# The last 512 tokens' gate projection moved between the Fourier products, and the attention tables loaded row by row

## The chip, the cores and the metric

The kernel runs on one core of a Trainium2 chip. The metric is the device time of one execution in microseconds, the median of three runs. All work of the core shares one TensorE (PE), one VectorE (DVE), one ScalarE (ACT), one GpSimd (POOL), the SyncE (SP), which in this kernel issues nearly all transfers, and 16 DMA engines.

## The reference

One layer of a hybrid encoder on 2048 tokens of 1024 channels, in float32, cut here to the parts that matter:

```python
h = rms_norm(x, norm1_g)
u_f, q, k, v, g = split(h @ w_in)                 # 512, 512, 512, 512, 2 x 1024 columns
g = sigmoid(g.reshape(b, s, 2, 1024) + b_gate)
a = fourier_mix(u_f) @ w_fa                       # real part of a 2-D DFT, 4 groups of 128 channels
n = neighbourhood_attention(q, k, v, rpb) @ w_nb  # 8 heads; window of 8 rows x 16 columns, with a bias table
x = x + (g[0] * a + g[1] * n) @ w_out
up = depthwise_conv(rms_norm(x) @ w_up); val, gate = split(up)
x = rms_norm(x + (silu(gate) * val) @ w_down)
```

## The kernel before

Five stages run one after the other with a barrier between them: input projection, Fourier mixing, attention, mixer output, feed-forward. Each stage is a block in which every engine has its own instruction list, written out by hand; order between engines is kept by semaphores alone. SP works through its list in order, and so a transfer waits for every wait that stands ahead of it in that list.

Every float32 product is made of three matmuls on a head and a tail (`SPLIT`): an operand is rounded to a head, and the tail is the operand less the head. Weights are read raw (512 KB a tile), DVE casts the head (`head`, L226, and L279 in the gate loop), and POOL subtracts for the tail (`tail`, L202).

**Input stage** (`input_phase`). The normalised, turned input stays in SBUF as `hT`, head and tail, 128 KB of each partition. The gates are the last part: 16 weight tiles of 128 output channels, each against four blocks of 512 tokens. One tile and block is 24 matmuls of 128x512 (`tile`, L357). ACT adds the bias and takes the sigmoid on the way from PSUM to a stage buffer (L335), and SP stores it to `gT` in HBM (L189). The loop over the gates is a hardware loop (`Fori`), two weight tiles a turn.

**Fourier stage** (`fourier_phase`). SP loads `u` in two halves of 256 columns, the position table (`traw`, 2 MB) and the channel table (L479 to L482). DVE does a 16-point transform of each half (`dft16`, L525 and L528); ACT and POOL split its result into `Y` (L620, L508). PE multiplies it by the position table, 48 matmuls of 128x256 for each group (L666); ACT and DVE split that into `X` (L628, L583); PE multiplies by the channel table, 18 matmuls (L676); ACT and DVE write the group's output (L635, L594, L599), and SP stores it (L495). SP's list also makes the shifted bias tables for the attention: a zeroed table, the `rpb` values put into it, and 48 small copies of 31 KB (L484 to L491).

**Attention stage** (`attention_phase`). For each of 8 heads SP loads q and k twice (4 x 512 KB), nine bias tables (9 x 256 KB, L785) and the values (16 x 64 KB, L793); for head 0 the window mask (2.3 MB, L787) stands between bias and values. ACT casts q and k (L883), POOL and DVE subtract for the tails (L819, L860), DVE adds the mask to each bias table (L857), and 128 tiles of scores follow: PE scores (L938), DVE adds the bias and takes the maximum (L836), ACT exponential (L889), PE transpose (L948), DVE copy (L844), PE values (L960).

Of the kernel before, what the change touches and what calls it, by code (L numbers as in the profile page):

```python
# [44 lines left out]

class Pool:
# [18 lines left out]
def input_phase(nc, x, w_in, norm_g, b_gate, eye, u_out, qT_out, v_out, kT_out, gT_out):  # L65
# [6 lines left out]
    with ExitStack() as ctx:  # L72
        m = Pool(nc, ctx, "in")
        hT = m.sb("hT", [P, 2, KD, SEQ], F32R)
# [8 lines left out]
        bias_now = m.sb("bias_now", [P, 2])  # L83
# [22 lines left out]
        bias_ready = m.sem("bias_ready")  # L106
        evac_done = m.sem("evac_done")
        stored = m.sems("stored", STAGES)

# [6 lines left out]
        free_at = [0, 0, 0, 0, 0, 0, 20, 24, 16, 16, 16, 16, 28, 32, 52, 56]  # L116
        ng_evac = 16 + 16 + 16 + 16
# [7 lines left out]
        def _(sp):  # L125
# [46 lines left out]
            def load_gate(t):  # L172
                sp.dma_start(wraw[:, t % RAW], w_in[16 + t]).then_inc(w_in_raw[t % RAW], 16)

            for q in range(4):
                if q >= 2:
                    sp.wait_ge(w_tail, UQVK + q - 2 - 1)
# [4 lines left out]
            with sp.Fori(0, NG // 2 - 1) as i:  # L182
                for j in range(2):
                    sp.wait_ge(w_tail, i * 2 + (UQVK + j + 1))
                    sp.dma_start(wraw[:, j], w_in[bass.ds(i * 2 + (18 + j), 1)].rearrange("o p k c -> (o p) k c")
                                 ).then_inc(w_in_raw[j], 16)
                    for b in range(NBLK):
                        sp.wait_ge(evac_done, i * 8 + (ng_evac + 4 * j + b + 1))
                        sp.dma_start(gT_out[bass.ds((i * 2 + j) * P, P), b * BLK:(b + 1) * BLK],  # L189
                                     stage[:, b]).then_inc(stored[b], 16)  # L190
            n = ng_evac + 4 * (NG - 2)
            for t in range(NG - 2, NG):
                for b in range(NBLK):
                    store(n, gT_out[t * P:(t + 1) * P, b * BLK:(b + 1) * BLK])
                    n += 1
            for s in range(STAGES):
                sp.wait_ge(stored[s], 16 * (n // STAGES))

        @block.gpsimd
        def _(pool):  # L200
# [4 lines left out]
            for t in range(UQVK):  # L205
                pool.wait_ge(w_head, t + 1)
                tail(t, slot[t])
            with pool.Fori(0, NG // 2) as i:
                for j in range(2):
                    pool.wait_ge(w_head, i * 2 + (UQVK + j + 1))  # L210
                    tail(j, 4 + j)

        @block.vector
        def _(dve):
# [7 lines left out]
            def head(t):  # L222
                dve.wait_ge(w_in_raw[t % RAW], 16 * (t // RAW + 1))
                if free_at[t]:
                    dve.wait_ge(mm_done, free_at[t])
                nc.vector.tensor_copy(w[:, 0, slot[t]], wraw[:, t % RAW]).then_inc(w_head, 1)  # L226
# [18 lines left out]
            def h_tails(t):  # L245
                for g in range(2):
                    dve.wait_ge(head_done, 2 * t + g + 1)
                    ks, at = slice(4 * g, 4 * g + 4), slice(t * P, (t + 1) * P)
                    nc.vector.tensor_tensor(hT[:, 1, ks, at], ps[:, 2 * (t % 2) + g].rearrange("p (k q) -> p k q", q=P),  # L249
                                            f32(hT[:, 0, ks, at]), ALU.subtract).then_inc(tail_done, 1)  # L250
# [20 lines left out]
            for t in range(6, UQVK):  # L271
                head(t)
            with dve.Fori(0, NG // 2) as i:
                for j in range(2):
                    dve.wait_ge(evac_done, i * 8 + (60 + 4 * j))
                    nc.vector.tensor_copy(bias_now[:, j:j + 1], gbias[:, bass.ds(i * 2 + j, 1)]).then_inc(bias_ready, 1)
                    dve.wait_ge(w_in_raw[j], i * 16 + 16 * (UQVK // 2 + 1))
                    dve.wait_ge(mm_done, i * 8 + (60 + 4 * j))
                    nc.vector.tensor_copy(w[:, 0, 4 + j], wraw[:, j]).then_inc(w_head, 1)  # L279

        @block.scalar
        def _(act):
# [17 lines left out]
            def h_heads(t):  # L300
                act.wait_ge(x_turned, t + 1)
                for g in range(2):
                    nc.scalar.activation(hT[:, 0, 4 * g:4 * g + 4, t * P:(t + 1) * P],
# [25 lines left out]
            with act.Fori(0, NG // 2) as i:  # L329
                for j in range(2):  # L330
                    act.wait_ge(bias_ready, i * 2 + (j + 1))
                    for b in range(NBLK):
                        act.wait_ge(mm_done, i * 8 + (ng_evac + 4 * j + b + 1))
                        act.wait_ge(stored[b], i * 32 + 16 * (ng_evac // 4 + j))
                        nc.scalar.activation(stage[:, b], ps[:, 4 * j + b], ACT.Sigmoid,  # L335
                                             bias=bias_now[:, j:j + 1]).then_inc(evac_done, 1)

        @block.tensor
        def _(pe):
            pe.wait_ge(const_in, 48)  # L340

            def slab(n, t):
# [3 lines left out]
                for k in range(KD):  # L346
                    for a, b in SPLIT:
                        last = nc.tensor.matmul(ps[:, bank(n)], hT[:, a, k, t * P:(t + 1) * P], w[:, b, 0:4, k],  # L348
# [4 lines left out]
            def tile(bank, s, b, first_wait):  # L353
                pe.wait_ge(evac_done, first_wait)
                for k in range(KD):
                    for a, c in SPLIT:
                        last = nc.tensor.matmul(ps[:, bank], w[:, a, s, k], hT[:, c, k, b * BLK:(b + 1) * BLK],  # L357
# [37 lines left out]
            with pe.Fori(0, NG // 2) as i:  # L395
                for j in range(2):
                    pe.wait_ge(w_tail, i * 2 + (UQVK + j + 1))
                    for b in range(NBLK):
                        tile(4 * j + b, 4 + j, b, i * 8 + (ng_evac + 4 * j + b - BANKS + 1))


# [17 lines left out]
def fourier_phase(nc, u, pos_table, chan_table, fnT_out, rpb, padded, shifted):  # L419
# [14 lines left out]
    CW = 256  # L434
# [6 lines left out]
    USES = XB + 6  # L441
    with ExitStack() as ctx:
# [9 lines left out]
        traw = m.sb("traw", [P, A, 2 * P])  # L452
        tab = m.sb("tab", [P, 2, A, 2 * P], F32R)
        craw = m.sb("craw", [P, 2, P])
        ctab = m.sb("ctab", [P, 2, 2, P], F32R)
        X = m.sb("X", [P, 2, 2 * XB, 2, P], F32R)
        real = m.sb("real", [P, 2, BLK])
        out = m.sb("out", [P, 1, SEQ])
        zero = m.sb("zero", [REL_R * 4, P])
        ps = m.banks()  # L460

        zeroed, filled, placed, shifted_done = (m.sem(x) for x in ("zeroed", "filled", "placed", "shifted_done"))
        tab_in, u_in = m.sem("tab_in"), m.sems("u_in", CHUNKS)
# [6 lines left out]
        stored = m.sem("stored")  # L470

# [5 lines left out]
        def _(sp):  # L477
            u_v = u.rearrange("(a b) c -> b a c", b=P)
            sp.dma_start(ub[:, 0], u_v[:, :, 0:CW]).then_inc(u_in[0], 16)  # L479
            sp.dma_start(craw[:, :], chan_table).then_inc(tab_in, 16)  # L480
            sp.dma_start(traw[:, :], pos_table).then_inc(tab_in, 16)
            sp.dma_start(ub[:, 1], u_v[:, :, CW:2 * CW]).then_inc(u_in[1], 16)  # L482
            sp.wait_ge(zeroed, 1)
            sp.dma_start(padded.rearrange("h r (x c) -> (h r x) c", x=1).rearrange("(p y) c -> p (y c)", y=2),  # L484
                         zero[:, :]).then_inc(filled, 16)
            sp.wait_ge(filled, 16)
            sp.dma_start(padded[:, PAD_R:PAD_R + RPB_R, PAD_C:PAD_C + RPB_C], rpb).then_inc(placed, 16)
            sp.wait_ge(placed, 16)
# [1591 lines left out]
```

## Time and profile before

| | us |
|---|---|
| median of the runs (lowest, highest) | 3009.2 (3006.93, 3011.0) |
| the profiled execution's own time | 3011.05 |
| span of its trace | 3009.2 |
| PE busy, share of the span | 2726.6, 91% |
| DVE / ACT / POOL busy | 1411.5 / 894.0 / 863.9 |
| input stage, by SP's first transfers | 0 to 742.67 |
| Fourier stage | 742.67 to 860.87 |
| attention, from its first transfer to its last product | 860.87 to 1176 |
| mixer output and feed-forward | 1176 to 3009.2 |

PE's share in forty equal slices of the span, in tenths, where 9 is 90% or more, and the clock that it was granted:

```profile
PE   6999999998238997899994999997999999999997
PEclk9999999999669998999997999998999999999999
```

Each slice is 75.2 us. PE is full in the first nine after the start, falls to 2 and 3 tenths in the tenth and the eleventh after that (slices 11 and 12, the Fourier stage and the beginning of the attention) and is full again from there, with three short dips.

### The profile page before, as it was taken

Reading aid. Unit: us, or ns where it says so; the run is one execution under the profiler, and the core shown is the slowest. Engines: PE = TensorE matmul, PEld = TensorE weight load, DVE = VectorE, ACT = ScalarE, POOL = GpSimd, SP = SyncE. Lnnn points to the kernel's source line nnn. Section 1 sums busy time; section 2 is a strip of 40 time slices with the busy share of each in tenths; the row PEclk is TensorE's granted clock in tenths of the full one; section 3 lists DMA queues with packets and bytes.
Section 4 is the critical chain, followed back from the end, with each engine's and each line's share of the span. In section 5 each row is a group of like instructions: output and inputs, shape, how many; then the busy total and the mean of one; then the engine's idle time right before and its main releaser. Section 6 shows DMA issues by size and latency. Waiting matters only on the chain. (4 is left out here: it accounts for less than half of the span.)

```text
span 3009.2 us, 34345 instructions
## 1 busy us (share of the span) xinstructions
PE 2726.6 (91%) x12792; PEld 2265.5 (75%) x12792; DVE 1411.5 (47%) x2231; ACT 894.0 (30%) x1598; POOL 863.9 (29%) x477
## 2 busy tenths in 40 slices
PE   6999999998238997899994999997999999999997
PEld 5888888886237885677873788886888887888886
DVE  4300000000838886643445899998655554131232
ACT  3211111111225663122113444444222223343332
POOL 1020001010312232532222666665000003554553
PEclk9999999999669998999997999998999999999999
DMA  4322122222257762665544777777666665554653
GB/s 138 95 95 71 61 69 77 70 72 90 78 142 175 187 179 87 196 184 165 183 137 158 266 279 275 275 275 244 218 223 220 221 223 196 180 198 147 204 174 112
DMA packets 242518, 499.29 MB, mean 166 GB/s; under 512 B 65476, under 2 KB 86720, under 8 KB 239040
## 3 DMA queue, kind: packets, MB, share of 16 engines
q1 hardware_dynamic: 223424, 480.52, 49.3%
q10 hardware_dynamic: 18944, 16.78, 1.6%
q8 instruction: 92, 1.51, 0.2%
q14 instruction: 58, 0.48, 0.0%
HBM read 326.24 MB, written 172.52 MB: 166 GB/s over the span
## 5 line engine op out<-in xcount | busy, mean ns | idle before, releaser
L357 PE MATMUL in_psum<-in_hT,in_w 128*128 128x512 f32 x2304 | 522.6, 389 | 0.0
L357 PEld LDWEIGHTS in_psum<-in_hT,in_w 128*128 128x128 f32 x2304 | 432.5, 188 | 89.8
L1999 PE MATMUL ff_psum<-ff_w,ff_hid 128*128 128x512 f32 x2112 | 479.5, 389 | 2.1 <-POOL ff_w L1591 2.0
L1999 PEld LDWEIGHTS ff_psum<-ff_w,ff_hid 128*128 128x128 f32 x2112 | 396.3, 188 | 85.2 <-POOL ff_w L1591 2.4
L1591 POOL TENSOR_TENSOR ff_w<-ff_st,ff_w 128x512 fp32r<-128x512 f32 x176 | 249.8, 1429 | 635.0 <-ACT ff_w L1835 634.6
L1591 POOL TENSOR_TENSOR ff_w<-ff_wraw,ff_w 128x512 fp32r<-128x512 f32 x154 | 270.5, 1758 | 239.4 <-ACT ff_w L1835 239.4
L1960 PE MATMUL ff_psum<-ff_h,ff_w 128*128 128x512 f32 x1056 | 247.5, 394 | 27.3 <-DVE ff_h L1658 27.1
L202 POOL TENSOR_TENSOR in_w<-in_wraw,in_w 128x1024 fp32r<-128x1024 f32 x32 | 77.1, 2413 | 622.1 <-DVE in_w L226 311.4
L1960 PEld LDWEIGHTS ff_psum<-ff_h,ff_w 128*128 128x128 f32 x1056 | 200.6, 190 | 70.7 <-POOL ff_w L1591 28.1
L1960 PE MATMUL ff_psum<-ff_h,ff_again 128*128 128x512 f32 x1056 | 244.9, 391 | 3.5 <-DVE ff_h L1658 3.5
L1960 PEld LDWEIGHTS ff_psum<-ff_h,ff_again 128*128 128x128 f32 x1056 | 199.3, 189 | 45.4 <-issue 3.9
L1256 PE MATMUL mo_psum<-mo_act,mo_w 128*128 128x512 f32 x768 | 190.0, 405 | 41.7 <-POOL mo_act L1107 22.0
L1716 DVE TENSOR_TENSOR ff_hid<-ff_kraw,ff_hid 128x1024 fp32r<-128x1024 f32 x44 | 55.2, 1254 | 328.8 <-ACT ff_hid L1877 328.7
L1256 PEld LDWEIGHTS mo_psum<-mo_act,mo_w 128*128 128x128 f32 x768 | 145.3, 193 | 84.0 <-POOL mo_w L1102 26.8
L1979 PE MATMUL ff_psum<-ff_h2c,ff_w 128*128 128x512 f32 x792 | 189.1, 397 | 13.5 <-POOL ff_w L1591 13.5
L1979 PE MATMUL ff_psum<-ff_h2c,ff_again 128*128 128x512 f32 x792 | 188.9, 397 | 8.3 <-DVE ff_h2c L1658 6.8
L1979 PEld LDWEIGHTS ff_psum<-ff_h2c,ff_w 128*128 128x128 f32 x792 | 152.0, 192 | 47.1 <-POOL ff_w L1591 15.2
L348 PE MATMUL in_psum<-in_w,in_hT 128*128 128x512 f32 x768 | 180.5, 394 | 5.8 <-DVE in_hT L249 5.8
L1979 PEld LDWEIGHTS ff_psum<-ff_h2c,ff_again 128*128 128x128 f32 x792 | 152.1, 193 | 41.6 <-issue 6.4
L1271 PE MATMUL mo_psum<-mo_wo,mo_mixed 128*128 128x512 f32 x768 | 177.4, 391 | 1.6 <-DVE mo_mixed L1163 1.6
L1862 ACT ACTIVATE ff_vg<-ff_c,ff_param 128x1024 f32<-128x1024 f32 x88 | 109.6, 1246 | 222.2 <-DVE ff_c L1682 191.4
L348 PEld LDWEIGHTS in_psum<-in_w,in_hT 128*128 128x128 f32 x768 | 144.5, 190 | 35.9 <-DVE in_hT L249 6.2
(167 smaller groups left out, 3448.5 us busy)
## 6 DMA issues: line engine op xcount, KB each, us to landing
split<-ff_w SPq DMA_DIRECT2D x154, 512.0 KB, 3.4
ff_again<-split SPq DMA_DIRECT2D x154, 512.0 KB, 4.0
ff_st<-in_w_down_dram SPq DMA_DIRECT2D x176, 256.0 KB, 3.0
ff_wraw<-in_w_up_dram SPq DMA_DIRECT2D x44, 512.0 KB, 5.5
hidden<-ff_c SPq DMA_DIRECT2D x44, 512.0 KB, 2.9
ff_kraw<-hidden SPq DMA_DIRECT2D x44, 512.0 KB, 4.6
at_bias<-shifted SPq DMA_DIRECT2D x72, 256.0 KB
in_wraw<-in_w_in_dram SPq DMA_DIRECT2D x32, 512.0 KB, 3.9
```

What stands on the lines that cost most here:

```text
L202: nc.gpsimd.tensor_tensor(w[:, 1, s], wraw[:, t % RAW], f32(w[:, 0, s]), ALU.subtract).then_inc(w_tail, 1)
L348: last = nc.tensor.matmul(ps[:, bank(n)], hT[:, a, k, t * P:(t + 1) * P], w[:, b, 0:4, k], start=(k == 0 and (a, b) == SPLIT[0]), stop=(k ...
L357: last = nc.tensor.matmul(ps[:, bank], w[:, a, s, k], hT[:, c, k, b * BLK:(b + 1) * BLK], start=(k == 0 and (a, c) == SPLIT[0]), stop=(k = ...
L1256: last = nc.tensor.matmul(ps[:, 2 * (n % 2) + branch], w[:, a, s % 2, k], act_s[:, c, k], start=(k == ks[0] and (a, c) == SPLIT[0]), stop= ...
L1271: last = nc.tensor.matmul(ps[:, 4 + half], mixed[:, a, k, t * P:(t + 1) * P], wo[:, c, k, half * SPH:(half + 1) * SPH], start=(k == 0 and ...
L1591: nc.gpsimd.tensor_tensor(split_out(i, 1), parts(i), f32(split_out(i, 0)), ALU.subtract).then_inc(w_tail, 1)
L1716: T.tensor_tensor(hid[:, 1, n % 2], kraw[:, :, :], f32(hid[:, 0, n % 2]), ALU.subtract).then_inc(k_tail, 1)
L1862: nc.scalar.activation((val, gate)[r], c[:, n % 2, r], ACT.Identity, scale=taps(t, 1), bias=taps(t, 3)).then_inc(centred, 1)
L1960: last = nc.tensor.matmul(bank(n, j), weights(i)[:, a, q * P:(q + 1) * P], h1[:, k, q, b], start=(k == 0 and (a, b) == SPLIT[0]), stop=(k ...
L1979: last = nc.tensor.matmul(bank(n, P2 + s), weights(i)[:, a, k * P:(k + 1) * P], h2c[:, s, k, b], start=(k == 0 and (a, b) == SPLIT[0]), st ...
L1999: last = nc.tensor.matmul(ps[:, 4 * (1 - half) + t], hid[:, a, (b * PAIRS + pair) % 2, q, t * P:(t + 1) * P], weights(i)[:, e], start=(r = ...
```

## The change

1. **Gates.** In the input stage the gate tiles are now multiplied with the first three token blocks only (`GB = 3`), in a written-out loop. The last block's `hT` lives in a buffer of its own, `hB`, which outlives the stage. Each split gate weight tile (head and tail, 1 MB) is stored to a new scratch `gate_w` in HBM.
2. **Fourier stage.** It reads the 16 split tiles back through a ring of three buffers (`gw`), and PE does the 16 missing tile-and-block products between the Fourier products, into two banks of PSUM kept for them; the Fourier products cycle through six banks (`FB`) instead of eight. `u` comes in four chunks of 128 columns, each with its own `dft16` just ahead of its group. ACT takes the sigmoids and stores them on its own queue.
3. **Attention.** The mask comes in nine pieces on ACT's queue, three of them first; the values of head 0 stand behind the first three bias tables instead of behind all nine and the mask; DVE starts on the first row of tables when that row is there; for head 0 ACT casts k ahead of q.
4. The feed-forward stage uses fewer semaphores for the same waits; `load_y` gets one more wait (for the loads before it). These are not shown.

```diff
 # input stage, SP
+            def store_gate_w(t):
+                sp.wait_ge(w_tail, UQVK + t + 1)
+                at_least(sp, gate_stored, 16 * t)
+                sp.dma_start(gate_w[t], f32(w[:, :, slot[UQVK + t]])).then_inc(gate_stored, 16)
...
+            for t in range(NG):
+                store_gate_w(t)
+                if t + 2 < NG:
+                    load_gate(t + 2)
+                for b in range(GB):
                     store(n, gT_out[t * P:(t + 1) * P, b * BLK:(b + 1) * BLK])
 # input stage, PE
-            with pe.Fori(0, NG // 2) as i:
-                for j in range(2):
-                    pe.wait_ge(w_tail, i * 2 + (UQVK + j + 1))
-                    for b in range(NBLK):
-                        tile(4 * j + b, 4 + j, b, i * 8 + (ng_evac + 4 * j + b - BANKS + 1))
+            for t in range(NG):
+                pe.wait_ge(w_tail, UQVK + t + 1)
+                for b in range(GB):
+                    tile(n % BANKS, slot[UQVK + t], b, n - BANKS + 1)
+                    n += 1
 # Fourier stage
-    CW = 256
+    CW = 128
+    FB = BANKS - 2
+    NG, GRING = 2 * KD, 3
...
+            def load_gate_w(t):
+                at_least(sp, gate_mm, t - GRING + 1)
+                sp.dma_start(f32(gw[:, t % GRING]), gate_w[t]).then_inc(gw_in[t % GRING], 16)
...
             dft16(0)
-            dft16(1)
             for g in range(FNET_GROUPS):
+                if g + 1 < CHUNKS:
+                    dft16(g + 1)
                 group(g)
 # Fourier stage, ACT
+            def gates(*tiles):
+                for t in tiles:
+                    act.wait_ge(gate_mm, t + 1)
+                    nc.scalar.activation(sig[:, t % 2], ps[:, FB + t % 2], ACT.Sigmoid,
+                                         bias=gbias[:, t:t + 1]).then_inc(gate_out, 1)
+                    act.wait_ge(gate_out, t + 1)
+                    at_least(act, gate_stored, 16 * t)
+                    act.dma_start(gT_out[t * P:(t + 1) * P, SEQ - BLK:SEQ], sig[:, t % 2]).then_inc(gate_stored, 16)
 # Fourier stage, PE
+            def gates(*tiles):
+                for t in tiles:
+                    pe.wait_ge(gw_in[t % GRING], 16 * (t // GRING + 1))
+                    at_least(pe, gate_out, t - 1)
+                    for k in range(KD):
+                        for a, b in SPLIT:
+                            last = nc.tensor.matmul(ps[:, FB + t % 2], gw[:, t % GRING, a, k], hB[:, b, k],
...
 # attention, SP, head 0
+                if h == 0:
+                    load_bias(0, 0)
+                    load_values(0)
+                    load_bias(0, 1)
+                    load_bias(0, 2)
+                    return
...
-                if h == 0:
-                    sp.dma_start(window[:, :], mask).then_inc(const_in, 16)
 # attention, DVE
-                dve.wait_ge(bias_in[h % 2], 16 * NB * (h // 2 + 1))
+                if h == 0 and kind < KINDS:
+                    dve.wait_ge(first_in, 32 * KINDS)
+                elif h % 2:
+                    dve.wait_ge(bias_in[1], 16 * NB * (h // 2 + 1))
+                else:
+                    dve.wait_ge(bias_in[0], 32 * (NB - KINDS) + 16 * NB * (h // 2))
 # attention, ACT
+            load_mask(0)
             for part in range(2 * PARTS):
-                qk_head(0, part)
+                qk_head(0, (part + PARTS) % (2 * PARTS))
+            load_mask(1)
+            load_mask(2)
```

PE's list in the Fourier stage, whose rows say line, operation, output and inputs, shape and count. Before, the first three groups:

```order
L666 MATMUL ft_psum<-ft_tab,ft_Y 128x256 x48
L676 MATMUL ft_psum<-ft_X,ft_ctab 128x512 x12
L676 MATMUL ft_psum<-ft_X,ft_ctab 128x128 x6
L666 MATMUL ft_psum<-ft_tab,ft_Y 128x256 x48
L676 MATMUL ft_psum<-ft_X,ft_ctab 128x512 x12
L676 MATMUL ft_psum<-ft_X,ft_ctab 128x128 x6
```

The same place of PE's list now, with `in_hB` the kept token block and `ft_gw` the ring of weights:

```order
L734 MATMUL ft_psum<-in_hB,ft_gw 128x512 x96
L749 MATMUL ft_psum<-ft_tab,ft_Y 128x256 x48
L734 MATMUL ft_psum<-in_hB,ft_gw 128x512 x24
L761 MATMUL ft_psum<-ft_X,ft_ctab 128x512 x12
L761 MATMUL ft_psum<-ft_X,ft_ctab 128x128 x6
L734 MATMUL ft_psum<-in_hB,ft_gw 128x512 x48
L749 MATMUL ft_psum<-ft_tab,ft_Y 128x256 x48
L734 MATMUL ft_psum<-in_hB,ft_gw 128x512 x48
L761 MATMUL ft_psum<-ft_X,ft_ctab 128x512 x12
L761 MATMUL ft_psum<-ft_X,ft_ctab 128x128 x6
L749 MATMUL ft_psum<-ft_tab,ft_Y 128x256 x48
```

Four gate tiles (96 matmuls) stand ahead of the first Fourier product, and one or two tiles between most others. Further down the list (not shown) the position products of the third and of the fourth group follow the channel product of the group before directly, and three tiles stand at the end.

SP's list at the start of the Fourier stage, before:

```order
L479 DMA ft_u<-u 128x16x256
L480 DMA ft_craw<-in_chan_table_dram 128x256
L481 DMA ft_traw<-in_pos_table_dram 128x4096
L482 DMA ft_u<-u 128x16x256
L484 DMA padded<-ft_zero 124x128
```

SP's list there now, down to the second batch of bias-table copies:

```order
L496 DMA ft_u<-u 128x16x128
L493 DMA ft_gw<-gate_w 128x2048
L509 DMA ft_craw<-in_chan_table_dram 128x256
L510 DMA ft_traw<-in_pos_table_dram 128x4096
L511 DMA ft_gbias<-in_b_gate_dram 128x16
L493 DMA ft_gw<-gate_w 128x2048
L496 DMA ft_u<-u 128x16x128
L493 DMA ft_gw<-gate_w 128x2048
L516 DMA padded<-ft_zero 124x128
L519 DMA padded<-in_rpb_dram 8x15x31
L496 DMA ft_u<-u 128x16x128 x2
L493 DMA ft_gw<-gate_w 128x2048
```

The second weight tile stands behind the 2 MB table, the fourth (the last row) behind two waits for the padded table and behind the last two chunks of `u`; 16 small copies then stand ahead of each of the next two.

SP's list at the start of the attention, before:

```order
L774 DMA at_kraw<-kT 64x2048
L785 DMA at_bias<-shifted 128x1x512 x9
L787 DMA at_window<-in_mask_dram 128x4608
L793 DMA at_vs<-v 32x8x64 x16
L774 DMA at_qraw<-qT 64x2048
```

And now:

```order
L894 DMA at_kraw<-kT 64x2048
L877 DMA at_bias<-shifted 128x1x512 x3
L884 DMA at_vs<-v 32x8x64 x16
L877 DMA at_bias<-shifted 128x1x512 x6
L894 DMA at_qraw<-qT 64x2048
```

The mask is gone from SP's list; it stands on ACT's. The number of bytes ahead of head 1's q and k (the last row) is the same over both queues.

## Rows read from the trace of the kernel before

**Rows 1.** Windows: from:to length, PE PEld DVE ACT POOL busy, clock, DMA share, GB/s.
```profile
0.00:739.00 739.00, 715.25 (x3200) 592.78 (x3200) 80.89 (x176) 132.21 (x217) 77.33 (x36) 1.00 0.24 80
742.67:789.45 46.78, 0.00 (x0) 0.00 (x1) 38.43 (x35) 7.75 (x4) 20.13 (x4) 0.50 0.55 163
789.45:857.00 67.55, 43.60 (x264) 39.55 (x264) 42.35 (x71) 19.80 (x34) 9.03 (x2) 0.82 0.16 53
860.87:882.60 21.73, 0.00 (x0) 0.00 (x0) 4.62 (x1) 5.55 (x9) 4.50 (x1) 0.50 0.81 182
882.60:924.00 41.40, 16.71 (x74) 14.05 (x75) 13.22 (x34) 8.29 (x22) 1.13 (x1) 0.60 0.79 179
```

**Rows 2.** Waits between 739 and 925 us.
```profile
PE ft_psum L666 <- POOL ft_Y L508: 50.5, 1, 50.5
PE at_psum L938 <- DVE at_kl L860: 28.4, 1, 28.4
PE ft_psum L676 <- DVE ft_X L583: 21.2, 4, 11.2
DVE at_bias L857 <- DMA at_window<-in_mask_dram: 18.5, 1, 18.5
```

**Rows 3.** The gate loop: its matmuls by line, then timeline rows of two weight tails.
```profile
L357 PE MATMUL in_psum<-in_hT,in_w 128*128 128x512 f32 x420 | 95.4, 389 | 0.0
...
653.72 2.40 POOL L202 TENSOR_TENSOR in_w<-in_wraw,in_w 128x1024 fp32r<-128x1024 f32 x1 [19.27 <-DVE in_w L279]
...
697.24 2.40 POOL L202 TENSOR_TENSOR in_w<-in_wraw,in_w 128x1024 fp32r<-128x1024 f32 x1 [19.27 <-DVE in_w L279]
```

**Rows 4.** Timeline (start, us, what) from the last gate to the Fourier end.
```profile
739.05 0.69 ACT L335 ACTIVATE in_stage<-in_psum,in_bias_now 128x512 f32<-128x512 f32 x1 [4.75 <-PE in_psum L357]
742.67 0.39 SPq L479 DMA_DIRECT2D ft_u<-u  x1
...
750.89 4.49 DVE L528 TENSOR_TENSOR ft_st<-ft_u 128x2048 f32<-128x2048 f32 x2 [7.96 <-DMA ft_u<-u]
756.77 0.42 ACT L612 ACTIVATE ft_ctab<-ft_craw 128x256 fp32r<-128x256 f32 x1 [17.03 <-DMA ft_traw<-in_pos_table_dram]
...
763.23 0.79 SPq L487 DMA_DIRECT2D padded<-in_rpb_dram  x1
765.55 31.59 SPq L491 DMA_DIRECT2D shifted<-padded  x48
...
843.21 5.95 PE L666 MATMUL ft_psum<-ft_tab,ft_Y 128*128 128x256 f32 x48
850.55 3.68 PE L676 MATMUL ft_psum<-ft_X,ft_ctab 128*128 128x512 f32 x18 [1.39 <-DVE ft_X L583]
```

**Rows 5.** Windows while PE worked again, and in its next pause.
```profile
793.00:795.00 2.00, 2.00 (x19) 2.00 (x18) 2.00 (x3) 0.60 (x1) 0.00 (x0) 0.97 0.31 49
801.00:805.00 4.00, 0.00 (x0) 0.00 (x0) 3.97 (x13) 0.00 (x0) 0.00 (x0) 0.50 0.00 0
```

**Rows 6.** ACT's and POOL's split of the transform, by line: count, busy us, mean ns.
```profile
L508 POOL TENSOR_TENSOR ft_Y<-ft_u,ft_Y 128x2048 fp32r<-128x2048 f32 x4 | 18.8, 4707 | 42.4 <-ACT ft_Y L620 42.4
...
L620 ACT ACTIVATE ft_Y<-ft_u 128x2048 fp32r<-128x2048 f32 x4 | 7.5, 1906 | 25.6 <-DVEq L557 12.2 <-DVEq L577 7.9 <-PE ft_psum L666 5.6
```

**Rows 7.** Timeline of the attention's start.
```profile
863.74 10.75 SPq L785 DMA_DIRECT2D at_bias<-shifted  x9
873.61 2.19 ACT L883 ACTIVATE at_qs<-at_qraw 128x512 fp32r<-128x512 f32 x4 [18.58 <-DMA at_kraw<-kT]
...
877.86 26.60 SPq L793 DMA_DIRECT2D at_vs<-v  x16
...
904.57 0.50 SPq L774 DMA_DIRECT2D at_qraw<-qT  x1
...
916.91 0.63 ACT L883 ACTIVATE at_qs<-at_qraw 128x512 fp32r<-128x512 f32 x1 [9.52 <-DMA at_kraw<-kT]
```

**Rows 8.** SP's timeline of head 7's values.
```profile
1114.25 17.75 SPq L793 DMA_DIRECT2D at_vs<-v  x16
```

More of the change, by code:

```diff
@@ L43, with at_least @@
 SPLIT = ((0, 0), (0, 1), (1, 0))
+def at_least(engine, sem, value):
+    if value > 0:
+        engine.wait_ge(sem, value)
 class Pool:
@@ L203, in tail @@
                                         ALU.subtract).then_inc(w_tail, 1)
-            for t in range(UQVK):
+            for t in range(UQVK + NG):
                 pool.wait_ge(w_head, t + 1)
                 tail(t, slot[t])
[L208 to L211, printed above, removed]
         @block.vector
@@ L270, in _ @@
                     head(4 + t)
-            for t in range(6, UQVK):
+            for t in range(6, UQVK + NG):
                 head(t)
[L273 to L279, printed above, removed]
         @block.scalar
@@ L328, in _ @@
                 n += 1
[L329 to L336, printed above, removed]
+            for t in range(NG):
+                for b in range(GB):
+                    evac(n, ACT.Sigmoid, bias=gbias[:, t:t + 1])
+                    n += 1
         @block.tensor
@@ L455, in fourier_phase @@
         ctab = m.sb("ctab", [P, 2, 2, P], F32R)
+        with ExitStack() as first:
+            traw = Pool(nc, first, "ft").sb("traw", [P, A, 2 * P])
         X = m.sb("X", [P, 2, 2 * XB, 2, P], F32R)
@@ L634, in group @@
                         act.wait_ge(mirror_done, n - 1)
[L635 removed]
+                    nc.scalar.activation(real[:, n % 2, 0:w * P], ps[:, (USES * g + XB + 2 * q) % FB, 0:w * P],
                                          ACT.Copy, scale=ORTHO).then_inc(real_done, 1)
[L638 to L642 removed]
+            def gates(*tiles):
[6 more added lines that the diff above has]
+                    act.dma_start(gT_out[t * P:(t + 1) * P, SEQ - BLK:SEQ], sig[:, t % 2]).then_inc(gate_stored, 16)
+            gates(0, 1)
+            heads(0)
+            gates(2, 3)
+            spectrum(0)
+            gates(4)
+            heads(1)
+            reals(0)
+            gates(5, 6)
+            spectrum(1)
+            gates(7, 8)
+            heads(2)
+            reals(1)
+            spectrum(2)
+            gates(9, 10)
+            heads(3)
+            reals(2)
+            spectrum(3)
+            gates(11, 12)
+            reals(3)
+            gates(13, 14, 15)
+            act.wait_ge(gate_stored, 16 * NG)
         @block.tensor
@@ L909, in turn, with load_mask @@
                     ps[:, TB].rearrange("p (j b c) -> p j b c", b=QR, c=QC)[:, :, ::-1], ACT.Copy).then_inc(evac, 1)
+            def load_mask(i):
+                for kind in range(i * KINDS, (i + 1) * KINDS):
+                    act.dma_start(window[:, kind], mask[:, kind]).then_inc(bias_in[0] if i else first_in, 16)
+            load_mask(0)
             for part in range(2 * PARTS):
-                qk_head(0, part)
+                qk_head(0, (part + PARTS) % (2 * PARTS))
+            load_mask(1)
+            load_mask(2)
             for n in range(-4, N + 1):
```

244 lines of the change are left out of this document (149 added, 95 removed).

## The prediction

> **What bounds the kernel now.** I read the page's forty slices first: PE is busy 91% of the span, so the time is PE's work plus the stretches in which it has none. Then the windows by stage. Up to 739 us PE is busy and at full clock [rows 1]. From SP's first Fourier transfer at 742.67 to 789.45 it does nothing; from there to 857 it works 43.6 of 67.6 us, at a mean clock of 0.82 of full; in the first 21.7 us of the attention it again does nothing, and in the next 41.4 it works 16.7. The reader should see there one stage with PE full and next to it two starts with PE empty. The waits name the causes: 50.5 us for the split of the first transform, 21.2 us in four waits for the spectrum's tails, 28.4 us at the attention's start and on DVE 18.5 us for the mask [rows 2]. The gate loop has no idle time at all (0.0 in its row), so what is taken from it comes off in full [rows 3].
>
> **What the input stage loses.** Two tails of gate weights two tiles apart begin at 653.72 and 697.24 us, so eight tile-and-block products take 43.52 us, 5.44 each [rows 3]. Sixteen go: 16 x 5.44 = 87.0 us. The additions hide under PE. A weight tile now lasts 3 x 5.44 = 16.3 us. The cast and tail of the next one start when the tile two before it is done; the tail takes 2.4 us [rows 3], so with a cast of 1 us at most some 13 us are spare. The store of a split tile (1 MB) stands on SP ahead of the next raw load and of three stage stores; DMA share is 0.24 in this stage [rows 1], and 17 MB more over the 48 x 5.44 = 261 us of gates adds 64 GB/s to the 80. ACT has four stage buffers of 5.44 us each before it would wait. If that cover failed, a late tile would cost the excess over 13 us. I take 0, from -2 (written-out code in place of a loop) to +5.
>
> **What the Fourier stage becomes.** I count from SP's first transfer there, T, at 742.67 before and at 742.67 - 87.0 = 655.7 now. Before, the next stage's first transfer came at 860.87, T + 118.2.
>
> PE's work is 16 x 5.44 = 87.0 us plus four groups of 5.95 + 3.68 = 9.63 us [rows 4], 38.5: together 125.5 at full clock. It used to hold 38.5. What comes on top:
>
> *Start.* The first 2.1 MB (`u`) were there 8.2 us after their issue, the channel table and the 2.1 MB position table at 14.1 us [rows 4]: 2.8 us for each MB and 2.5 fixed. `u` now comes in pieces of 512 bytes where they had 1024, and no row of before has such a load into SBUF. Bounds: 2.8 us a chunk of 1 MB if bytes decide, and 8.8 if pieces cost what the values' pieces of 256 bytes do (17.7 us for 1 MB and thus 4096 of them, [rows 8]). Keeping the pace of pieces that `u` had gives 5.6. I take 4.4, between the two nearest. First gate weight at 2.5 + 4.4 + 2.8 = T + 9.7; second, behind 0.4 + 5.6 us of tables, at 18.5; third, behind `u`'s second chunk, at 25.7. Then SP stops until the zeroed table is written (about 26), puts in `rpb`, and only then issues two chunks of `u` and the fourth weight: 26.7 + 2.5 + 8.8 + 2.8 = 40.8.
>
> The Trainium skill, "DMA: Bandwidth & Descriptors", Specifications, puts line rate at pieces of 512 bytes and more. By that rule a chunk costs 2.8 us, the fourth weight comes at 34.4, and the total below falls by 6.4 us. No row of before decides it.
>
> *Clock.* After some 50 us without work PE began at the lower level, 1.2 GHz, and was back at 0.97 in the window of 793 to 795, some 4 us later; in the pause that followed it was at 0.50 again by 801 [rows 5]. A restart thus costs about 2 us. I count two: the first tile, and the fourth, which waits from 31.1 on.
>
> *Gates 0 to 3.* 9.7 + 7.4 = 17.1; 18.5 + 5.4 = 23.9; 25.7 + 5.4 = 31.1; 40.8 + 7.4 = 48.2. Lost: 9.7 at the start, 4.0 of clock, 1.4 + 1.8 + 9.7 = 12.9 of waits.
>
> *The rest.* With position product 0 PE is at 54.2. The fifth and sixth weights stand behind 16 small copies each, at 31.59 / 48 = 0.66 us [rows 4] 10.5 us a batch: issued near 39 and 50, there near 45 and 56, wanted at 54 and 63. From then on a weight is issued when the tile three before it is done and needs 2.5 + 2.8 = 5.3 us, while PE has two tiles (10.9 us) to do: covered. Not covered are the splits of chunks 2 and 3: their casts stand on ACT behind the sigmoid of the gate tile just ahead, and behind them ACT has the real parts that free the banks. With casts of two times 1 us and tails of two times 2.4 on POOL (half of those before, [rows 6]), position product 2 can start about 6 us after gates 8 ended, of which the channel product covers 3.7; the same for group 3. I take 2.5 each, 5 together, between 0 and 12. DVE was busy 38.4 + 42.4 us in the two windows [rows 1] and has 157 now, so the transforms of the later chunks lie beside gate tiles. Sum: 9.7 + 125.5 + 4.0 + 12.9 + 5.0 = T + 157.1 for PE's last matmul. The last sigmoid, its store and the barrier take what they took before between the end of the last gate matmul (739.05) and the next stage's first transfer (742.67) [rows 4], 3.6 us: T + 160.7, so the stage grows from 118.2 to 160.7, by 42.5. Net of the 87.0: **44.5 us gained**.
>
> **Attention.** No instruction on an engine's steady path changes. Before, all 7.9 MB that DVE needs for its second row of tables, and 2 MB more for head 1's q and k, go through one queue in a row: q and k of head 0 are there 12.7 us after the first issue at 860.87, SP spends 10.75 us on bias tables and 26.6 on the values, with the mask in front of them [rows 7], where the values of a later head take 17.75 [rows 8]. Head 1's q and k are issued at 904.57 and there at 916.91; ACT waits for them, and everything behind it. That moment is what counts: 56.0 us after the stage's start. Now three mask pieces run beside q and k, which makes these about 3 us later, and DVE's mask wait at 901 becomes one at about 883. But the same 10 MB must pass before head 1 can be cast. The stretch had a DMA share of 0.81 and 0.79 [rows 1]; two queues may fill it. At a share of 1 the 56 us would become 45, a gain of 11; with no better filling it is 0, and the later start of q and k can make it -3. I take 5, the middle of these.
>
> Against that speaks the Trainium skill, "DMA: Bandwidth & Descriptors", section "Issuing engines are not separate DMA queues": transfers of all issuing engines share the same DMA engines, and a second one saves only issue time. By it the 5 us would be near 0; it is the first rival.
>
> Everything else (feed-forward's semaphores) I take at 0: the new wait in `load_y` is for the loads of a block earlier, which that block's own additions have already waited for.
>
> **Sum.** 3011.05, the profiled execution's own time, - 44.5 - 5 = 2961.6. The median stood 1.9 lower than that execution, so 2960.
>
> **Rivals.**
> 1. *The attention start is bound by bytes.* For it: share near 0.8 at only 180 GB/s [rows 1]. Against: SP's 26.6 us for values that take 17.75 elsewhere. Time 2965 to 2968.
> 2. *The ring starves PE.* Each refill waits on SP behind stores that wait for DVE's output. If the ten tiles from the sixth on come 2 us late each, 20 us are gone: 2980. For it: one list, in order, with waits on three engines. Against: 10.9 us of cover for 5.3.
> 3. *Faster.* `u` in pieces of 512 bytes runs at full rate (6.4 us), the later products don't wait (5), attention gains 9: 2944 to 2950.
> 4. *Slower than before: PE stays at the lower clock through the Fourier stage*, because product, gate and wait alternate. At a granted clock of 0.50 the 125.5 us become 251, of which 4 are in the sum already, and the time is 2960 + 121 = 3081. It decides from 49 us of full-rate work done at half rate on. For it: a mean clock of 0.82 there before [rows 1]. Against: what lowered it were pauses of 7 us and more, and my list has one such behind the start.
> 5. *The change does nothing*, since the weights come back so late that all that PE saved is waited for: 3009. It would take 49 us more of waiting than I found.
>
> **Chances.** Forecast (2953 to 2973, less rival 1) 0.50; rival 1 0.18; rival 2 (2973 to 2990) 0.16; rival 3 0.12; rival 4 0.02; rival 5 0.02. `u` at its slow bound moves the fourth weight by 17.6 us and so belongs with rival 2's times. The range of 2946 to 2984 leaves out the ends of rivals 2 and 3 and all of 4 and 5. This kernel can be told from no change at about 0.2%, 6 us: faster 0.96, same 0.02, slower 0.02.
>
> **What would show it.** After: gate tiles 5.44 us apart with no idle in the input stage, and SP's first Fourier transfer near 655.7; gates 0 to 3 starting near T + 10, 18.5, 26 and 41; clock 1.00 from the first position product on; no wait for weights after the fourth tile above 1 us; PE's last Fourier-stage matmul near T + 157, T + 161 for the next stage; head 1's cast about 51 us after that. I am wrong if the first Fourier transfer comes after 662, if waits for `gate_w` beyond the fourth tile add up to over 10 us, if the clock is below 0.9 in the stage's second half, or if the attention takes longer from its first transfer to its end than 315 us.

## The result, and the profile after

The changed kernel took 2984.65 us (median of 4 runs, 2978.5 to 2988.89) against 3008.84 us before: a ratio of 0.992, 95% interval 0.9901 to 0.994. It is faster by 24 us (0.8%), half of the 49 forecast, and its time lies 0.65 us above the upper end of the range. The profiled execution is the shortest of the four: 2978.5 us, span 2976.7.

By stage, with each stage's start taken from SP's first transfer in it (us; "again" is a second trace of the same kernel, taken in the first set of experiments):

| | before | forecast | after | again |
|---|---|---|---|---|
| Fourier stage begins | 742.67 | 655.7 | 652.46 | 654.33 |
| its length | 118.2 | 160.7 | 178.2 | 178.6 |
| attention, to the mixer's first transfer | 322.3 | 317 | 324.3 | 324.6 |
| mixer output | 427.6 | as before | 424.7 | 430.3 |
| feed-forward | 1398.4 | as before | 1397.1 | 1397.3 |

The gates left the input stage at the pace forecast. The stage ends 3.2 us earlier than forecast in this trace and 1.4 in the second; over the nine traces with the changed input stage it is 1.1 to 3.6. Some 2.5 of the 3.2 lie ahead of the gates: the first product of the input projection starts at 25.21 us, where it was 27.66. In windows of the trace after (as [rows 1]: from:to length, busy us of PE, PEld, DVE, ACT, POOL, clock, DMA share, GB/s) the input stage, the wait for the first weight, PE's stretch in the Fourier stage, and the attention's first two stretches:

```profile
0.00:648.90 648.90, 627.58 (x2816) 520.32 (x2816) 79.63 (x160) 113.25 (x194) 77.16 (x36) 1.00 0.33 111
652.46:661.88 9.42, 0.00 (x1) 0.01 (x1) 2.80 (x4) 0.00 (x0) 0.00 (x0) 0.51 0.94 318
661.88:827.06 165.18, 137.64 (x648) 116.07 (x648) 77.30 (x166) 38.06 (x57) 30.65 (x10) 0.88 0.56 182
830.64:854.83 24.19, 0.00 (x0) 0.03 (x1) 4.90 (x2) 5.55 (x9) 4.52 (x1) 0.50 0.97 221
854.83:892.00 37.17, 14.27 (x57) 11.35 (x58) 11.50 (x30) 6.63 (x17) 0.00 (x0) 0.59 0.74 146
```

The third row is where the gain went: PE has work for 125.5 us at full clock there, takes 165.2, and its mean clock is 0.88. Weight tiles in the gate loop's trace follow each other at 16.3 us, three products of 5.44, with no idle time of PE, as [rows 3]:

```profile
L362 PE MATMUL in_psum<-in_hA,in_w 128*128 128x512 f32 x434 | 98.5, 389 | 0.0
```

PE's timeline in the Fourier stage after (start, us, what, idle before), the part that answers to the last two of [rows 4]:

```profile
661.88 13.58 PE L734 MATMUL ft_psum<-in_hB,ft_gw 128*128 128x512 f32 x48 [13.00 <-DMA ft_gw<-gate_w]
675.64 5.73 PE L734 MATMUL ft_psum<-in_hB,ft_gw 128*128 128x512 f32 x24 [0.18 <-DMA ft_gw<-gate_w]
691.72 8.26 PE L734 MATMUL ft_psum<-in_hB,ft_gw 128*128 128x512 f32 x24 [10.35 <-DMA ft_gw<-gate_w]
699.82 5.92 PE L749 MATMUL ft_psum<-ft_tab,ft_Y 128*128 128x256 f32 x48
705.58 5.63 PE L734 MATMUL ft_psum<-in_hB,ft_gw 128*128 128x512 f32 x24
711.04 3.50 PE L761 MATMUL ft_psum<-ft_X,ft_ctab 128*128 128x512 f32 x18
717.23 7.36 PE L734 MATMUL ft_psum<-in_hB,ft_gw 128*128 128x512 f32 x24 [2.68 <-DMA ft_gw<-gate_w]
729.79 7.99 PE L734 MATMUL ft_psum<-in_hB,ft_gw 128*128 128x512 f32 x24 [5.20 <-DMA ft_gw<-gate_w]
...
761.56 7.47 PE L749 MATMUL ft_psum<-ft_tab,ft_Y 128*128 128x256 f32 x48 [3.79 <-POOL ft_Y L553]
...
788.62 7.78 PE L749 MATMUL ft_psum<-ft_tab,ft_Y 128*128 128x256 f32 x48 [5.34 <-POOL ft_Y L553]
...
810.48 16.58 PE L734 MATMUL ft_psum<-in_hB,ft_gw 128*128 128x512 f32 x72
```

The reader should see two things. Six pauses stand out: the first one (13.00, of which 9.4 lie in this stage), three for weights behind the third (10.35, 2.68, 5.20), and two for the split of the third and fourth transform (3.79, 5.34). And behind each pause the next row is longer than its like without one: 7.36, 7.99 and 8.26 us where 5.63 is a tile's length, 7.47 and 7.78 where 5.92 is a position product's.

SP's timeline of the same stretch shows why the sixth and the seventh weight were late (the fifth was in time):

```profile
677.75 2.61 SPq L496 DMA_DIRECT2D ft_u<-u  x2
680.40 4.33 SPq L493 DMA_DIRECT2D ft_gw<-gate_w  x1
684.77 13.81 SPq L500 DMA_DIRECT2D shifted<-padded  x16
698.62 0.47 SPq L493 DMA_DIRECT2D ft_gw<-gate_w  x1
699.14 11.48 SPq L500 DMA_DIRECT2D shifted<-padded  x16
710.66 0.47 SPq L493 DMA_DIRECT2D ft_gw<-gate_w  x1
711.18 13.02 SPq L500 DMA_DIRECT2D shifted<-padded  x16
724.24 1.42 SPq L493 DMA_DIRECT2D ft_gw<-gate_w  x3
```

The sixth tile's weight (index 5) is issued at 710.66 and PE begins with it at 717.23; the seventh's at 724.24, begun at 729.79. Each stands behind a batch of 16 copies, and the three batches hold SP for 11.5 to 13.8 us each. From 718.3 to 724.0, with copies alone in SP's queue, the DMA engines are busy 0.30 of the time at 47 GB/s: it isn't their load that keeps the seventh weight back.

ACT's casts in the attention, of head 0's k and of head 1's q, as the two of [rows 7]:

```profile
845.87 0.63 ACT L1000 ACTIVATE at_kh<-at_kraw 128x512 fp32r<-128x512 f32 x1 [18.08 <-DMA at_kraw<-kT]
...
888.21 0.63 ACT L1000 ACTIVATE at_qs<-at_qraw 128x512 fp32r<-128x512 f32 x1 [26.67 <-DMA at_kraw<-kT]
```

Head 1's cast is 57.6 us after the stage's start, where it was 56.0.

### The profile page after: what moved, and what is told of

The parts are those of the page before. It is cut to its first block and busy times, and to the rows that moved or that the text cites. A ratio compares the mean times of both kernels' runs of the same rounds, so it can differ in the third digit from the quotient of the medians.

```text
span 2976.7 us, 33988 instructions
## 1 busy us (share of the span) xinstructions
PE 2729.0 (92%) x12792; PEld 2268.5 (76%) x12792; DVE 1406.7 (47%) x2279; ACT 886.5 (30%) x1595; POOL 871.4 (29%) x481
## 5 line engine op out<-in xcount | busy, mean ns | idle before, releaser
L362 PE MATMUL in_psum<-in_hA,in_w 128*128 128x512 f32 x1728 | 393.1, 389 | 0.0
L362 PEld LDWEIGHTS in_psum<-in_hA,in_w 128*128 128x128 f32 x1728 | 324.4, 188 | 67.2
L1709 POOL TENSOR_TENSOR ff_w<-ff_wraw,ff_w 128x512 fp32r<-128x512 f32 x154 | 279.4, 1816 | 231.8 <-ACT ff_w L1953 231.7
L242 DVE CAST in_w<-in_wraw 128x1024 fp32r<-128x1024 f32 x32 | 22.8, 717 | 482.9 <-PE in_psum L362 415.7
L1374 PEld LDWEIGHTS mo_psum<-mo_act,mo_w 128*128 128x128 f32 x768 | 143.7, 191 | 82.4 <-POOL mo_w L1220 25.7
L1953 ACT ACTIVATE ff_w<-ff_st 128x512 fp32r<-128x512 f32 x176 | 109.5, 628 | 231.1 <-PE ff_psum L2117 214.8
```

Source lines behind the costliest of these rows:

```text
L362: last = nc.tensor.matmul(ps[:, bank], w[:, a, s, k], hT(c, k, b * BLK, BLK), start=(k == 0 and (a, c) == SPLIT[0]), stop=(k == KD - 1 and ...
L1374: last = nc.tensor.matmul(ps[:, 2 * (n % 2) + branch], w[:, a, s % 2, k], act_s[:, c, k], start=(k == ks[0] and (a, c) == SPLIT[0]), stop= ...
L1709: nc.gpsimd.tensor_tensor(split_out(i, 1), parts(i), f32(split_out(i, 0)), ALU.subtract).then_inc(w_tail, 1)
L1953: nc.scalar.activation(split_out(i, 0), parts(i), ACT.Copy).then_inc(w_head, 1)
```

## The experiments

Each was timed in five rounds with the kernel before; the medians of before in the three sets were 3010.15, 3008.51 and 3008.5 us.

**The changed kernel once more** (no edit).

> The changed kernel once more, as the control of this set. Its four executions so far lay between 2978.5 and 2988.9 us, those of before between 3006.9 and 3011.0, and its one trace is that of the shortest. If the spread is that of the chip, this set gives 2978 to 2989 again, with the Fourier stage within 1 us of 178.2 in a second trace and the difference elsewhere. If the Fourier stage itself varies (its transfers race with the products), a second trace shows it several us longer or shorter.

Measured: 2983.63 us (2980.55 to 2986.95), ratio 0.9905, interval 0.9887 to 0.9923. The Fourier stage took 178.6 us against 178.2, the attention 324.6 against 324.3; the mixer output, which the change doesn't touch, took 430.3 against 424.7. In the eleven traces of this case it lay between 423.3 and 430.3 us. So 5.6 of the 8.4 us between the two traces' spans are there, and the Fourier stage's length repeats. The single waits in it repeat less well: 5.56 and 4.75 us for the sixth and the seventh weight, where it was 2.68 and 5.20. What makes the mixer stage vary wasn't looked into.

**The gates alone.** The edit gives the changed kernel the attention stage of before:

```diff
-def attention_phase(...)   # as changed
+def attention_phase(...)   # as before
```

> The changed kernel with the attention stage of before. Theory A (the attention's start moves 10 MB through DMA engines that are near full, so the new order gains nothing): within 3 us of the changed kernel, attention stage 322 us where the changed one has 324. Theory B, the prediction's (the new order gains 5 us): 5 us slower than the changed kernel.

Measured: 2979.81 us (2977.44 to 2982.71), ratio 0.9893, interval 0.9875 to 0.9911, 3.8 us below the changed kernel in the same set; attention stage 322.3 us. The prediction's theory, 5 us slower, falls: the attention's new order gains nothing that can be seen. By the traces it costs 2 us on average: the stage took 322.1 to 322.3 us in the three traces with the old order, and 320.9 to 328.4, on average 324.1, in the seven with the new one. The intervals of the two ratios overlap, so 3.8 is not a firm number.

**The attention's order alone.** The kernel before with the changed attention stage.

> The kernel before with the attention stage of the changed one. Theory A: 3009 to 3012 us, head 1's first cast 56 to 58 us after the stage's first transfer, as in both traces. Theory B: 3004 us.

Measured: 3008.86 us (3002.44 to 3015.3, 12 runs), ratio 0.9991, interval 0.9979 to 1.0002. No change that can be measured. In its trace head 1's first cast came 58.8 us after the stage's first transfer (919.35 - 860.53) and the stage took 328.4 us, the longest of all. The times alone don't decide here: the interval also holds the 5 us of theory B (a ratio of 0.9983). The trace speaks for theory A.

**The copies spread.** SP's list in the Fourier stage:

```diff
             load_gate_w(3)
-            sp.wait_ge(padded_in, 32)
-            shift(0)
             load_gate_w(4)
-            shift(1)
             load_gate_w(5)
-            shift(2)
+            sp.wait_ge(padded_in, 32)
+            shift_some(8)
             for t in (6, 7, 8):
                 load_gate_w(t)
+                shift_some(5)
...                                   # likewise behind weights 9 to 13
```

> The changed kernel with the 48 small copies of the bias tables taken from ahead of the fifth, sixth and seventh gate weight: the fifth and sixth are issued right behind the fourth, and the copies follow in groups of 8 and then 5 behind each later weight. Theory A (SP's list delays the weights): the waits of 2.7 and 5.2 us for weights 5 and 6 and the slow clock behind them (1.9 and 2.5 us) go, the Fourier stage falls from 178 to about 166, the time by 12. Theory B (the weights are late because the DMA engines are busy with other bytes): the copies delay the later weights as much, and the time stays within 3 us.

(Where this text says "weights 5 and 6" it counts from 0; the waits of 2.7 and 5.2 us are those of the sixth and the seventh.) Measured: 2974.43 us (2972.96 to 2976.33), ratio 0.9879, interval 0.9861 to 0.9896: 9.2 us below the changed kernel in the same set. The stage took 167.45 us (653.40 to 820.85), 10.7 less. PE's timeline, from the fifth gate tile on:

```profile
706.64 5.63 PE L737 MATMUL ft_psum<-in_hB,ft_gw 128*128 128x512 f32 x24
712.11 3.50 PE L764 MATMUL ft_psum<-ft_X,ft_ctab 128*128 128x512 f32 x18
715.44 11.14 PE L737 MATMUL ft_psum<-in_hB,ft_gw 128*128 128x512 f32 x48
...
750.57 8.49 PE L752 MATMUL ft_psum<-ft_tab,ft_Y 128*128 128x256 f32 x48 [3.98 <-POOL ft_Y L556]
```

The sixth and seventh tile run in one row of 11.14 us, with no wait ahead of or between them. The stage still moves the same bytes; it was SP's list that made the two weights late. The gain is a little smaller than the 12 us expected: the two products behind the splits took 8.49 and 8.29 us here, where the changed kernel's took 7.47 and 7.78.

**Splits earlier**, on top of that. ACT's list in the Fourier stage:

```diff
-            gates(7, 8)
+            gates(7)
             heads(2)
+            gates(8)
             reals(1)
             spectrum(2)
-            gates(9, 10)
+            gates(9)
             heads(3)
+            gates(10)
             reals(2)
```

> On top of the kernel with the copies spread: ACT casts the third and the fourth transform's output between the two sigmoids ahead of it (sigmoid 7, cast, sigmoid 8, and 9, cast, 10) and not behind both. There the position products of groups 2 and 3 waited 4.0 and 5.0 us and then ran 2.5 us slower each. Theory A (ACT's order makes the wait): the split is ready 5 us sooner, both waits and the slow clock go, stage 167.4 - 13 = 154 to 155 us, time 13 less (about 2962). Theory B (the banks, freed by the group before, are the real limit): a wait of 2 to 4 us stays in each, stage 161 or more.

Measured: 2963.13 us as the median of six runs. One of them took 4358.71 us at a mean granted clock of 0.597, where the others had 0.962 to 0.966; nothing here explains it. Without it the median is 2961.63; the comparison leaves it out: ratio 0.9848, interval 0.9835 to 0.986. The stage took 154.6 us, 12.9 less. The two position products:

```profile
746.23 5.98 PE L754 MATMUL ft_psum<-ft_tab,ft_Y 128*128 128x256 f32 x48 [0.74 <-DVE ft_out L647]
...
768.17 5.98 PE L754 MATMUL ft_psum<-ft_tab,ft_Y 128*128 128x256 f32 x48 [1.71 <-DVE ft_out L647]
```

What is left (0.74 and 1.71 us) waits for the banks, DVE's output of the group before. Theory A holds, up to these 2.5 us: the banks were second, as theory B had it, but 3 us behind.

**The fourth weight earlier**, on the kernel with the copies spread:

```diff
             load_gate_w(2)
+            load_gate_w(3)
             sp.wait_ge(step, 1)
...
             load_u(3)
-            load_gate_w(3)
```

> On top of the kernel with the copies spread: the fourth gate weight is issued ahead of the zeroed table, its wait and the last two chunks of u. There PE waited 10.6 us for it and lost 2.5 of clock. Theory A (the list's order makes the wait): the weight lands about 26 to 30 us after the stage's start in place of 39, PE waits at most 1 us for it, but the first position product then waits for its split (there 34.4 us after the start in the changed kernel), so 10 to 12 us less in all: stage 156. Theory B (the queue's bytes decide): the weight lands only 3 us sooner.

Measured: 2960.83 us (2958.55 to 2967.14), ratio 0.9846, interval 0.9832 to 0.9859. The stage took 154.6 us, 12.9 less:

```profile
675.26 11.18 PE L737 MATMUL ft_psum<-in_hB,ft_gw 128*128 128x512 f32 x48 [0.20 <-DMA ft_gw<-gate_w]
687.23 5.98 PE L752 MATMUL ft_psum<-ft_tab,ft_Y 128*128 128x256 f32 x48 [0.80 <-POOL ft_Y L556]
```

The third and the fourth tile run without a pause, and the first position product waits 0.80 us for its split.

**All three, with the attention of before.**

> Copies spread, splits earlier, fourth weight earlier, and the attention of before. If the three waits of the Fourier stage are separate, their gains add: stage 178.2 - 10.7 - 13 - 11 = 143.5 us against the 135 us of PE's work and the first weight's landing; with 2 to 4 us for the attention, 2984 - 35 - 3 = 2946. If one hides another, 2955 or more.

Measured: 2948.53 us (2945.96 to 2952.42), ratio 0.9805, interval 0.9793 to 0.9818. The stage took 145.4 us and the attention 322.1. One by one the edits took 10.7, 12.9 and 12.9, together 32.8, not 36.5. Some 1.5 of the missing 3.7 us are in the two products behind the splits: the edit on the splits took them from 8.49 and 8.29 to 5.98 each, but with the fourth weight earlier they took only 7.48 and 7.81, so that less was left to gain. Another 1.1 is the slow stretch of the fourth tile: it was 7.21 us long in place of 8.26 in the trace with the splits earlier, and that counts as a gain of both edits. Waits of 0.91, 0.98, 0.60 and 1.72 us are left. This version is faster than both kernels, by 60 us than the one before and, by the ratios, by 30 to 35 than the changed one.

**Less of the mask**, on the changed kernel: the mask's second and third row aren't loaded, and their tables are masked with the first row's, so this part of the result is another computation.

```diff
-                V.tensor_tensor(b, b, window[:, kind], ALU.add)
+                V.tensor_tensor(b, b, window[:, kind % KINDS], ALU.add)
...
-            load_mask(1)
-            load_mask(2)
```

> The changed kernel without the mask's second and third row (1.5 MB); their tables are masked with the first row's in their place. Theory A (the attention's start is bound by what passes the DMA engines): at 10 MB in 57 us, head 1's first cast comes about 8 to 9 us earlier (48 to 49 us after the stage's first transfer where it was 57.6), and so does the stage's end. Theory B (the order of SP's list, 24 us of which the values take): the values' issue takes its 24 us as before and head 1's cast comes within 2 us of 57.6.

Measured: 2971.33 us (2966.89 to 2976.41), ratio 0.9882, interval 0.9867 to 0.9896. Head 1's first cast came 49.9 us after the stage's first transfer in place of 57.6, and the stage took 316.2 us in place of 324.3. Both lie outside what the seven traces with all of the mask and this order gave (54.8 to 58.8, and 320.9 to 328.4). The rest of the gain in time isn't the mask's: the Fourier stage took 175.6 us in this trace and the mixer output 423.3. SP's timeline of the values and that cast:

```profile
833.62 18.05 SPq L884 DMA_DIRECT2D at_vs<-v  x16
```

```profile
878.59 0.63 ACT L1000 ACTIVATE at_qs<-at_qraw 128x512 fp32r<-128x512 f32 x1 [19.18 <-DMA at_kraw<-kT]
```

With 1.5 MB less, the values are issued in 18.05 us, as those of a later head [rows 8], where the changed kernel took 23.87; so the 24 us that I had read as SP's order were the queue's answer to bytes. Theory A: the moment depends on how much passes, not on the order.

**Filler**, on the kernel with the copies spread: work without use ahead of the two waits for the splits.

```diff
+                if g >= 2:
+                    t = (9, 11)[g - 2]
+                    pe.wait_ge(gate_out, t - 1)
+                    for i in range(12):
+                        nc.tensor.matmul(ps[:, FB + t % 2], ctab[:, 0, 0], hB[:, 0, i % KD],
+                                         start=True, stop=True)
                 pe.wait_ge(y_tail, 2 * g + 2)
```

> The kernel with the copies spread, in which the position products of groups 2 and 3 waited 4.0 and 5.0 us for their split and then took 8.5 and 8.3 us in place of 5.9. Here PE does 12 matmuls of 128x512 without use (into the bank that the next gate tile starts anew) ahead of each of the two waits: 2.7 us that fit into the pause. Theory A (the pause lowers PE's clock, and that costs as much again): the remaining waits are 1.3 and 2.3 us, the products take 5.9 to 6.0 us, and the Fourier stage falls from 167.4 to about 163. Theory B (the products are slow for another reason, as their operands' late arrival): stage 167.4, products over 8 us as before.

Measured: 2963.75 us (2962.25 to 2969.08), ratio 0.9854, interval 0.9836 to 0.9873, 10.7 us below the kernel without the filler, or 7.5 by the ratios, since the two were timed in different sets. The stage took 160.9 us, 6.6 less:

```profile
746.60 2.98 PE L748 MATMUL ft_psum<-in_hB,ft_ctab 128*128 128x512 f32 x12
750.93 6.01 PE L758 MATMUL ft_psum<-ft_tab,ft_Y 128*128 128x256 f32 x48 [1.35 <-POOL ft_Y L556]
...
771.03 2.98 PE L748 MATMUL ft_psum<-in_hB,ft_ctab 128*128 128x512 f32 x12
775.23 6.02 PE L758 MATMUL ft_psum<-ft_tab,ft_Y 128*128 128x256 f32 x48 [1.21 <-POOL ft_Y L556]
```

Without the filler, in the same place, the windows around the wait and the product show the clock (the third number from the end) fall to its lower level, 1.2 GHz (0.50), and come back:

```profile
746.00:750.50 4.50, 0.59 (x6) 0.44 (x4) 3.26 (x4) 1.90 (x4) 4.47 (x2) 0.88 0.80 249
750.00:752.00 2.00, 1.43 (x7) 1.46 (x8) 2.00 (x4) 0.00 (x0) 0.47 (x1) 0.50 0.30 90
754.00:757.00 3.00, 3.00 (x19) 3.00 (x19) 2.93 (x10) 0.60 (x1) 0.00 (x0) 0.62 0.04 14
757.00:759.00 2.00, 2.00 (x19) 2.00 (x18) 1.96 (x11) 0.86 (x2) 0.00 (x0) 1.00 0.00 0
```

With 24 useless matmuls PE finishes earlier: the products take 6.0 us in place of 8.5 and 8.3, 4.8 of the 6.6 us. That the pause lowers the clock, and that this cost 2.5 and 2.3 us here, is shown, not only read. The loss isn't the same each time: behind pauses of 3.8 and 4.0 us for the same split the same product took 7.47 us in one trace and 8.49 in another. What sets it wasn't found.

## Why the prediction was wrong

The direction and the main mechanism held: 16 products (87.0 us) left a full stage, and part of them came to lie where PE had had nothing to do. But the Fourier stage grew by 60.0 us and not by 42.5, and the attention by 2.0 us where a gain of 5 was forecast. The profiled execution gained 32.5 us where 49.5 was forecast. The 17.0 between are 17.5 for the Fourier stage and 7.0 for the attention, less 3.2 at the end of the input stage and 4.3 in mixer output and feed-forward. These last 7.5 us were not forecast (the 3.2 lie beyond the 2 us that I had allowed), and in part they are the luck of this one execution, for the median gained only 24. In the prediction's own steps, with T the stage's start:

- *Start*: right. First weight at T + 9.4 (forecast 9.7), third tile at T + 23.2 (25.7), fourth at T + 39.3 (40.8), first position product at T + 47.4 (48.2). One chunk of `u` in pieces of 512 bytes was there at T + 6.8, where 2.5 + 4.4 = 6.9 had been taken. By the line rate that the Trainium skill ("DMA: Bandwidth & Descriptors", Specifications) gives for 512 bytes on, the estimate would be T + 5.3. This one chunk, the only one that can be read by itself, came 1.5 us later than that; but a weight of 1 MB stood right behind it in the queue, and one reading doesn't decide.
- *The rest, weights*: **this step failed.** It had the fifth and sixth weight issued near T + 39 and T + 50, and every later one covered. The two were issued at T + 46.2 (still in time) and T + 58.2 (too late), and the seventh, for which the step named no copies at all, at T + 71.8 behind a third batch. The copies were priced at 10.5 us a batch from [rows 4] and took 13.8, 11.5 and 13.0, with the fourth weight's own issue held for 4.3 us ahead of them. Cost: 2.68 + 5.20 = 7.9 us of waits, and 10.3 in the second trace, beyond the 10 that I had named as a sign of being wrong. The experiment with the copies spread shows the cause. The text on the change named two batches ahead of the next two weights and stopped there; SP's list has a third right below.
- *The rest, splits*: the place was right, the size off. Waits of 3.79 and 5.34 us, 9.1 for the 5 forecast, within the 0 to 12 named. The cause named, ACT's sigmoids ahead of the cast, is shown by the experiment on the splits.
- *Clock*: **the second step that failed.** It was counted for two pauses of about 10 us and put at nothing for the short ones. Pauses of 2.7 to 5.3 us cost it too: 1.7 + 2.4 us behind the weights (7.36 and 7.99 against 5.63) and 1.5 + 1.9 behind the splits (7.47 and 7.78 against 5.92), 7.5 in all. For the two behind the splits the filler shows that it is the pause; for the two behind the weights that is taken over from there. I had argued against rival 4 that only pauses of 7 us and more lowered the clock before; nothing in the trace had shown that shorter ones, of 2.7 to 5.3 us, don't. I had also named a clock below 0.9 in the stage's second half as a sign; there it was 0.94, so that sign didn't show the cost.
- Sum: 7.9 + 4.1 + 7.5 = 19.5 us over the forecast, less 0.8 at the start and about 1 in products that ran a little shorter than 5.95 and 3.68, is about the 17.5 by which PE's last matmul (T + 174.6) was later than T + 157.1.
- *Attention*: the sign was wrong. I took the middle between -3 and 11 where the first rival said that bytes bind. The DMA share rose at first (0.97 over the first 24 us, where the first 22 had had 0.81) and fell behind that. Over the first 56 us of the stage it was 0.86 where it had been 0.83, and what was moved was 179 GB/s where it had been 183: the same 10 MB. So the moment that counts came no earlier. Leaving out 1.5 MB took 7.7 us off it, near the 8 to 9 worked out from 10 MB in 57 us. With the first rival stood the Trainium skill ("DMA: Bandwidth & Descriptors", "Issuing engines are not separate DMA queues"): a second issuing engine saves issue time only. The traces agree, with head 1's cast at 57.6 us after 56.0. The sign that I had set, over 315 us to the stage's last product, could not tell: it was 319.3 us now, but 317.4 before (the last product ends at 1178.2 and not at 1176).
- *Rivals*: rival 2 was the one that came, with a price near its 20 us, but not by its mechanism: the late weights stood behind the copies, while those behind the stores were all in time. Rival 1 came as well. Two rivals of 0.16 and 0.18 could happen together, and the range was built as if they excluded each other; both together end at about 2985. That the measured 2984.65 lies so near to it is in part luck, for the input stage's gain and the slow stretches are in neither. (From the sixth tile on there are eleven and not ten, so rival 2's own sum is 22 us.)

The mixer output, which the change doesn't touch, alone varied by 7.0 us between the eleven traces. Such a spread is part of a range too.

## What to carry to other kernels

When products are moved into the gaps of another stage, the gaps are worth only as much as the issuing list allows: go through that list row by row, batch by batch to its end, and give every transfer that is needed the time at which its turn comes, not the time at which its bytes could be there. Count each remaining pause of PE of a few microseconds about one and a half times, for the slow stretch that follows it: here 17.0 us of such pauses cost 7.5 us more. Before reordering transfers at a start that waits for them, add up what passes until the moment that counts: here the new order left the same 10 MB at the same 180 GB/s and gained nothing, and 1.5 MB fewer gained 7.7 us.

## What the runs showed of the hardware

- After pauses of 2.7 to 5.6 us PE ran at its lower level for a time, and rows of 5.6 to 5.9 us took 1.4 to 2.7 us more, over all traces; 3.0 us of useless matmuls in a pause of 4 to 5 us took this away and left pauses of 1.2 and 1.4, behind which the products took 6.0 us.
- A copy of 31 KB from HBM to HBM held SP for 0.66 us before, with nothing else in the queue (DMA share 0.29), and for 0.72 to 0.86 us with weights of 1 MB around it.
- The time from issue to use of head 1's q and k was 12.3 us in the old order and 25.1 us (863.11 to 888.21) in the new one: an earlier issue into a full queue only moved the wait.
